# The experts of a mixture layer taken in an order computed on the chip, with the first pass taken out of the loops

## The reference, cut to what matters

```python
def moe_ffn(h, w_router, b_router, w_gate_up, b_gate_up, w_down, b_down):
    logits = (xt @ w_router + b_router).astype(jnp.float32)
    top_val, top_idx = lax.top_k(logits, TOP_K)              # 4 of 32
    gates = jax.nn.softmax(top_val, axis=-1)
    ...
    def expert_block(args):
        xb, e = args
        gu = xb @ w_gate_up[e] + b_gate_up[e]                # 1024 -> 2048
        gate = jnp.minimum(gu[:, :D_FF], SWIGLU_LIMIT)
        up = jnp.clip(gu[:, D_FF:], -SWIGLU_LIMIT, SWIGLU_LIMIT)
        act = (up + 1) * gate * jax.nn.sigmoid(gate * SWIGLU_ALPHA)
        return act @ w_down[e] + b_down[e]                   # 1024 -> 1024
    ...
    out = jnp.zeros_like(xt).at[sorted_tok].add(contrib)     # times the gate
```

## Time and profile before

| what | before |
|---|---|
| median of three runs | 1321.47 us (1320.93 to 1327.84) |
| profiled execution | 1323.31 us |
| its span in the trace | 1321.6 us |
| TensorE busy | 1251.1 us, 95% |
| VectorE busy | 488.0 us, 37% |
| ScalarE busy | 251.9 us, 19% |
| GpSimd busy | 43.6 us, 3% |
| moved by DMA | 436.31 MB |

### The profile page before, as it was taken

The page is one execution under the profiler, slowest core; times in us unless marked ns, Lnnn a source line. Parts: engine busy times, 40 slices in busy tenths (PEclk is TensorE's granted clock), DMA queues, the critical chain, the costliest instruction groups (busy, mean ns, idle before and its releaser), DMA issues.

```text
span 1321.6 us, 17005 instructions
## 1 busy us (share of the span) xinstructions
PE 1251.1 (95%) x6399; PEld 545.0 (41%) x6400; DVE 488.0 (37%) x961; ACT 251.9 (19%) x440; POOL 43.6 (3%) x66
## 2 busy tenths in 40 slices
PE   5999999997999999999999999998899999999996
PEld 4665654653433343334333433333333333343332
DVE  2623544465423342334233432232233223342334
ACT  2031124462111111111111111111111111111112
POOL 2000003402000000000000000000000000000000
PEclk9989999997999999999999999999999999999998
DMA  9513126135999566994999999999999988999994
GB/s 322 205 64 129 64 80 215 42 127 216 427 428 428 234 282 271 429 428 194 429 428 428 428 428 428 428 428 428 428 428 428 428 343 362 429 428 428 428 428 201
DMA packets 43400, 436.31 MB, mean 330 GB/s; under 512 B 5717, under 2 KB 6861, under 8 KB 18806
## 3 DMA queue, kind: packets, MB, share of 16 engines
q1 hardware_dynamic: 39376, 429.41, 77.8%
q0 software_dynamic: 2080, 6.48, 1.5%
q10 hardware_dynamic: 1926, 0.18, 0.1%
HBM read 432.33 MB, written 3.72 MB: 330 GB/s over the span
## 4 chain that ended last, share of the span: by engine, by line
PE 70%; DMA 25%; DVE 3%; issue 1%; ACT 0%; ACTq 0%; SPq 0%; DVEq 0%
PE PS L1739 28%; DMA ring<-in_w_gate_up_dram 24%; PE PS L1774 12%; PE PS L1259 7%; PE PS L1268 5%; PE PS L1701 4%; PE PS L1221 3%; PE PS L1673 3%; PE PS L1270 1%; PE PS L1555 1%; PE PS L1727 1%; PE PS L1529 1%; PE PS L1410 1%; PE PS L1396 1%; DMA gffn<-in_norm_ffn_g_dram 1%
## 5 line engine op out<-in xcount | busy, mean ns | idle before, releaser
L1739 PE MATMUL PS<-ring,r 128*64 128x512 f32 x2304 | 523.5, 598 | 30.6 <-DMA ring<-in_w_gate_up_dram 30.6
L1739 PEld LDWEIGHTS PS<-ring,r 128*64 128x64 f32 x2304 | 158.6, 137 | 337.9 <-issue 274.2
L1774 PE MATMUL PS<-ring,r 128*64 128x512 f32 x1152 | 255.1, 595 | 0.2
L1134 DVE SCALAR_TENSOR_TENSOR r<-PS,gprev,r 128x512 f32<-128x512 f32 (+1 forms) x222 | 152.4, 741 | 119.3 <-PE PS L1701 119.3
L1774 PEld LDWEIGHTS PS<-ring,r 128*64 128x64 f32 x1152 | 82.2, 137 | 148.2 <-issue 148.2
L1200 DVE TENSOR_TENSOR yy<-PS,yy 128x512 fp32r<-128x512 f32 x36 | 24.9, 692 | 253.2 <-ACT yy L731 253.2
L722 ACT ACTIVATE r<-r 128x512 f32<-128x512 f32 x36 | 22.7, 630 | 492.0 <-DVE r L1186 492.0
L1186 DVE TENSOR_SCALAR r<-PS 128x512 f32<-128x512 f32 x36 | 24.9, 692 | 233.1 <-PE PS L1739 233.1
L1221 PE MATMUL PS<-ident,r 128*128 128x128 f32 (+5 forms) x490 | 81.6, 297 | 14.3 <-DMA gffn<-in_norm_ffn_g_dram 11.9
L1259 PE MATMUL PS<-r,ring 128*128 128x323 f32 x320 | 88.9, 435 | 0.2 <-DVE r L769 0.2
L1221 PEld LDWEIGHTS PS<-ident,r 128*128 128x128 f32 (+5 forms) x490 | 62.2, 183 | 39.6 <-issue 19.7
(11 more groups left out here) (293 smaller groups left out, 763.7 us busy)
## 6 DMA issues: line engine op xcount, KB each, us to landing
ring<-in_w_gate_up_dram SPq DMA_DIRECT2D x128, 2048.0 KB, 18.2
ring<-in_w_down_dram SPq DMA_DIRECT2D x64, 2048.0 KB, 18.1
ring<-in_w_in_dram SPq DMA_DIRECT2D x8, 2048.0 KB, 18.4
ring<-in_w_out_dram SPq DMA_DIRECT2D x3, 2048.0 KB, 7.7
r<-in_x_prompt_dram SPq DMA_DIRECT2D x2, 512.0 KB, 4.0
r<-in_x_prompt_dram POOLq DMA_DIRECT2D x2, 512.0 KB, 5.1
r<-bias_table_clipped SPq DMA_DIRECT2D x4, 256.0 KB, 7.1
out_dram<-r SPq DMA_DIRECT2D x2, 512.0 KB, 2.7
```

The lines of the kernel that those rows point to most:

```text
L1134: v.scalar_tensor_tensor(xx, PS[0:rows, out_banks(t)[h], :], gprev[0:rows, t:t + 1], xx, ALU.mult, ALU.add)\
L1739: last = mm(PS[64 * h:64 * h + 64, m, :], xt[:, k % 4, k // 4, :], w[:, kk, D * m + 512 * h:D * m + 512 * h + 512], start=False, stop=(k = ...
L1774: last = mm(PS[64 * h:64 * h + 64, 2, :], at[:, kk, c, :], w[:, kk, 512 * h:512 * h + 512], start=(c == 0 and kk == 0), stop=(c == 1 and k ...
```

## The change

Five edits stand in it.

1. **Order of the experts.** VectorE computes a key for each expert and its rank among the keys (`turn_no`). With m experts of more than 64 tokens (`many`; m = `many_to` at its end), the i-th expert that has not more gets the key i (m + 1), the j-th that has more gets j (33 - m) + 0.5, and expert 0 gets 0. One matmul with `ones` brings blocks and numbers of the experts into the order of the turns (`by_turn`); `order` holds the expert of each turn, `before` now the blocks before each turn, `turn_of` the turn of each block. SyncE's loop reads `order[n]` and `before[n]`; TensorE waits for the weights by turn.
2. **First pass outside the loops.** On TensorE, VectorE and ScalarE the loop's body is a function, and its first pass is written out with constants (expert 0, block 0). TensorE no longer waits for `route_ready` ahead of it. In this pass `combine` stands behind the third chunk instead of the first, and the transposes of the tables (three rows now) and of the gates stand behind the first and the second chunk. `gathered(0)` on VectorE moves ahead of the tables' second half, and `route_ready` comes ahead of the gates.
3. **Casts.** `top_four` compares with the integer indices themselves; `ix` is gone.
4. **Small loads.** `gffn4` is loaded behind the bias table, and counts on `head_in`.
5. **Start.** VectorE normalises the first two row tiles ahead of `par`, and TensorE transposes the first tile ahead of the wait for `gain_in`.

The diff, cut to its core (scratch views of `spare`, semaphore names and buffers are left out):

```diff
@@ -44,7 +44,7 @@
 EXPERT_SLOT = (1, 2, 3, 4, 0, 5)
-N_GAIN, N_HEAD, N_LATE = 7, 5, 4
+N_GAIN, N_HEAD, N_LATE = 6, 6, 4
 PART_ROWS = (0, 64, 96)
@@ -320,8 +330,9 @@
             used = ["gs_used", "gs_used1", "gs_used2", "gu_mm", "ds_used", "d_mm"]
-            with sp.Fori(1, NE) as e:
-                first = sp.value_load(before[0:1, bass.ds(e, 1)], min_val=1, max_val=MAX_BLOCKS)
+            with sp.Fori(1, NE) as n:
+                e = sp.value_load(order[0:1, bass.ds(n, 1)], min_val=0, max_val=NE - 1)
+                first = sp.value_load(before[0:1, bass.ds(n, 1)], min_val=1, max_val=MAX_BLOCKS)
                 for c in range(GU_CHUNKS + DN_CHUNKS):
@@ -470,7 +481,6 @@
             gain(praw[40:88, :], conv_w[0].rearrange("j (k p) -> (j k) p", p=128))
-            gain(gffn4[:, :, :], norm_ffn_g[0].rearrange("(h p k) -> p h k", h=2, p=128))
             act.dma_start(hraw[0:3], state_conv[0, 0]).then_inc(s["cvhist_in"], 16)
@@ -483,6 +493,7 @@
             head(tab[:, :], rel_bias_table[0])
+            head(gffn4[:, :, :], norm_ffn_g[0].rearrange("(h p k) -> p h k", h=2, p=128))
             head(wdt[:, :, :], w_in[0].rearrange("(k p) n -> p k n", p=128)[:, :, C_DT:C_DT + HEADS])
@@ -715,9 +726,8 @@
             a.activation(place[:, 0:TC], PS[:, 4, 0:TC], ACT.Copy).then_inc(s["c_ready"], 1)
-            act.wait_ge(s["route_ready"], 1)
-            total = act.value_load(blocks[0:1, 0:1], min_val=NE, max_val=MAX_BLOCKS)
-            with act.Fori(0, total) as b:
+            def expert_pass(b):
...
                 act.wait_ge(s["g_ready"], b + 1)
@@ -729,6 +739,12 @@
                 a.activation(yy2[:, 0, :], bank(2), ACT.Copy).then_inc(s["yy_ready"], 1)
...
+            expert_pass(0)
+            act.wait_ge(s["route_ready"], 1)
+            total = act.value_load(blocks[0:1, 0:1], min_val=NE, max_val=MAX_BLOCKS)
+            with act.Fori(1, total) as b:
+                expert_pass(b)
             for t in range(NT):
@@ -761,10 +774,14 @@
             normalised(0)
+            normalised(1)
+            dve.wait_ge(s["par_mm"], 1)
+            v.tensor_copy(par[:, :], PS[:, 7, 0:88]).then_inc(s["par_ready"], 1)
+            dve.wait_ge(s["par_ready"], 1)
             for i in range(6):
                 t, h, rows = i // 2, i % 2, ROWS[i // 2]
-                if h == 0 and t + 1 < NT:
-                    normalised(t + 1)
+                if i == 2:
+                    normalised(2)
                 dve.wait_ge(s["hT_mm"], i + 1)
@@ -1051,9 +1068,8 @@
                 step(v.max_index(i8[:, t, :], m8[:, t, :], lg[:, t, :]))
-                step(v.tensor_copy(ix[:, t, :], i8[:, t, :]))
                 step(v.tensor_tensor(eq[:, t, :, :], bc(iota[:, 0:NE].unsqueeze(1), 128, TOPK, NE),
-                                     bc(ix[:, t, 0:TOPK].unsqueeze(2), 128, TOPK, NE), ALU.is_equal))
+                                     bc(i8[:, t, 0:TOPK].unsqueeze(2), 128, TOPK, NE), ALU.is_equal))
                 for at0 in range(0, 128, rows):
@@ -1138,18 +1154,47 @@
-            count, nb, upto = PS[:, 2, 0:NE], nbk[:, 0, :], nbk[:, 1, :]
-            step(v.tensor_scalar(nb, count, float(CAP), 1.0, ALU.is_gt, ALU.add))
+            count, key, nb = PS[:, 2, 0:NE], key_nb[:, 0, :], key_nb[:, 1, :]
+            step(v.tensor_scalar(many, count, float(CAP), None, ALU.is_gt))
+            step(v.tensor_scalar(nb, many, 1.0, None, ALU.add))
             for m in range(2, TC // CAP):
                 step(v.scalar_tensor_tensor(nb, count, float(CAP * m), nb, ALU.is_gt, ALU.add))
-            step(v.tensor_tensor_scan(upto, nb, nbk[:, 3, :], 0.0, ALU.add, ALU.add))
-            step(v.tensor_scalar(nbk[:, 2, :], upto, pidx[:, 0:1], None, ALU.is_le))
-            step(v.tensor_tensor(nbk[:, 3, :], nbk[:, 2, :], nb, ALU.mult))
-            step(v.tensor_reduce(bej[:, :], nbk[:, 2:4, :], axis=X, op=ALU.add))
+            step(v.tensor_tensor_scan(many_to, many, zeros32, 0.0, ALU.add, ALU.add))
+            step(v.tensor_scalar(n_few, many_to[:, NE - 1:NE], -1.0, float(NE + 1), ALU.mult, ALU.add))
+            step(v.tensor_scalar(n_many, many_to[:, NE - 1:NE], 1.0, None, ALU.add))
+            step(v.tensor_tensor(few, rank[:, 0:NE], many_to, ALU.subtract))
+            step(v.tensor_scalar(few, few, n_many, None, ALU.mult))
+            step(v.tensor_scalar(key, many_to, n_few, 0.5, ALU.mult, ALU.add))
+            step(v.tensor_tensor(key, key, few, ALU.subtract))
+            step(v.tensor_tensor(key, key, many, ALU.mult))
+            step(v.tensor_tensor(key, key, few, ALU.add))
+            step(v.memset(key[:, 0:1], 0.0))
+            step(v.tensor_tensor(own, key_nb, bc(ident[:, 0:NE].unsqueeze(1), 128, 2, NE), ALU.mult))
+            step(v.tensor_reduce(own_key, own, axis=X, op=ALU.add))
+            step(v.tensor_scalar(few, key, own_key[:, 0:1], None, ALU.is_lt))
+            step(v.tensor_reduce(turn_no, few, axis=X, op=ALU.add))
+            step(v.tensor_scalar(at_turn[0:NE, 0, :], iota[0:NE, 0:NE + 1], turn_no[0:NE], own_key[0:NE, 1:2],
+                                 ALU.is_equal, ALU.mult))
+            v.tensor_scalar(at_turn[0:NE, 1, :], iota[0:NE, 0:NE + 1], turn_no[0:NE], pidx[0:NE],
+                            ALU.is_equal, ALU.mult).then_inc(s["turns_ready"], 1)
+            gathered(0)
+            dve.wait_ge(s["turns_mm"], 1)
+            step(v.tensor_copy(by_turn, PS[:, 2, 64:66 + 2 * NE].rearrange("p (a e) -> p a e", a=2)))
+            step(v.tensor_tensor_scan(upto, by_turn[:, 0, 0:NE], zeros32, 0.0, ALU.add, ALU.add))
+            step(v.tensor_tensor(few, by_turn[:, 1, 1:NE + 1], by_turn[:, 1, 0:NE], ALU.subtract))
+            step(v.tensor_scalar(done[:, 0, :], upto, pidx[:, 0:1], None, ALU.is_le))
+            step(v.tensor_tensor(done[:, 1, :], done[:, 0, :], by_turn[:, 0, 0:NE], ALU.mult))
+            step(v.tensor_tensor(done[:, 2, :], done[:, 0, :], few, ALU.mult))
+            step(v.tensor_reduce(bej[:, :], done, axis=X, op=ALU.add))
             v.tensor_tensor(bej[:, 1:2], pidx[:, :], bej[:, 1:2], ALU.subtract).then_inc(s["bej_ready"], 1)
-            step(v.tensor_tensor(nb[0:1], upto[0:1], nb[0:1], ALU.subtract))
-            step(v.tensor_copy(before[:, :], nb[0:1]))
+            step(v.tensor_tensor(few[0:1], upto[0:1], by_turn[0:1, 0, 0:NE], ALU.subtract))
+            step(v.tensor_copy(before[:, :], few[0:1]))
+            step(v.tensor_copy(order[:, :], by_turn[0:1, 1, 0:NE]))
             step(v.tensor_copy(blocks[:, :], upto[0:1, NE - 1:NE]))
+            dve.wait_ge(s["bej_mm"], 1)
+            step(v.tensor_scalar(turn_of[:, :], PS[0:1, 7, 0:128], float(NE - 1), None, ALU.min))
+            step(v.tensor_scalar(place_of[:, :], PS[0:1, 7, 128:256], 0.0, None, ALU.max))
+            v.tensor_copy(expert_of[:, :], PS[0:1, 7, 256:384]).then_inc(s["route_ready"], 1)
             dve.wait_ge(s["pv_ready"], 1)
@@ -1158,21 +1203,17 @@
             step(v.tensor_copy(pg[:, :, NT:2 * NT].rearrange("p e t -> p t e"), gates4[:, :, 0, :]))
-            dve.wait_ge(s["bej_mm"], 1)
-            step(v.tensor_scalar(expert_of[:, :], PS[0:1, 7, 0:128], float(NE - 1), None, ALU.min))
-            v.tensor_scalar(place_of[:, :], PS[0:1, 7, 128:256], 0.0, None, ALU.max).then_inc(s["route_ready"], 1)
             dve.wait_ge(s["route_ready"], 1)
             dve.sem_inc(s["o_ev"], 2)
-            gathered(0)
-            total = dve.value_load(blocks[0:1, 0:1], min_val=NE, max_val=MAX_BLOCKS)
             dve.wait_ge(s["c_ready"], 1)
...
             dve.sem_inc(s["yyl_ready"], 1)
-            with dve.Fori(0, total) as b:
-                e = dve.value_load(expert_of[0:1, bass.ds(b, 1)], min_val=0, max_val=NE - 1)
...
+            def expert_pass(b, e):
...
                 e_next = dve.value_load(expert_of[0:1, bass.ds(b + 1, 1)], min_val=0, max_val=NE - 1)
@@ -1199,6 +1240,11 @@
                     .then_inc(s["yyl_ready"], 1)
...
+            expert_pass(0, 0)
+            total = dve.value_load(blocks[0:1, 0:1], min_val=NE, max_val=MAX_BLOCKS)
+            with dve.Fori(1, total) as b:
+                expert_pass(b, dve.value_load(expert_of[0:1, bass.ds(b, 1)], min_val=0, max_val=NE - 1))
             dve.wait_ge(s["gates_held"], total + 2)
@@ -1222,11 +1268,11 @@
-            pe.wait_ge(s["gain_in"], N_GAIN * 16)
-            tr(PS[:, 7, 0:88], praw[:, :]).then_inc(s["par_mm"], 1)
...
             for i in range(6):
                 t, h, rows = i // 2, i % 2, ROWS[i // 2]
+                if i == 2:
+                    pe.wait_ge(s["gain_in"], N_GAIN * 16)
+                    tr(PS[:, 7, 0:88], praw[:, :]).then_inc(s["par_mm"], 1)
                 pe.wait_ge(s["xnorm"], t + 1)
@@ -1703,22 +1751,21 @@
-            gather(0)
-            pe.wait_ge(s["bej_ready"], 1)
-            for c in range(2):
-                last = tr(PS[0:1, 7, 128 * c:128 * c + 128], bej[:, c:c + 1])
-            last.then_inc(s["bej_mm"], 1)
-            turn(0)
-            places(0)
```

(39 more changed lines are left out.)

27 lines of the change are left out of this document (18 added, 9 removed).

## The result

| | before | after |
|---|---|---|
| median, first comparison (4 runs each) | 1322.76 us | 1309.17 us (1307.18 to 1309.51) |
| ratio, with its 95% interval | | 0.9888 (0.9858 to 0.9919) |
| the same again, 7 runs before and 4 after | 1325.39 us | 1309.58 us, ratio 0.9892 (0.9873 to 0.9911) |
| the same again, 9 runs before and 4 after | 1326.11 us | 1309.10 us, ratio 0.9876 (0.9858 to 0.9894) |
| profiled execution, span | 1323.31, 1321.6 us | 1308.86, 1307.1 us |

The change is a gain of 1.1 to 1.2%. The sign and the way in which the order works came as predicted, the size did not: 20.3 us were predicted, 14.5 us lie between the two spans, and 1309.2 us is outside the range, which ended at 1306.5.

A forecast was written before the change was run, and what follows sets the result against it. The prediction saw two limits, TensorE at 26.5 us a block and DMA at 29.4 us an expert. Order -20.5 and later first refill +0.2 gave -20.3, from 1321.5 to 1301.2 us; range 1296 to 1306.5.

The forecast's parts named there:

- What bounds it; the order: Expert passes: TensorE 26.5 us a block, DMA 29.4 us an expert; each two-block expert's second block frees five passes.
- The term of 20.5 us: Expert passes: spreading the two-block experts cuts losses from 36.4 to 15.9 us, saving 20.5 us.
- so passes 1 to 5 are free: Start of the expert passes: pass 0 counts as a second block, so passes 1 to 5 lose nothing.
- From R to pass 5, 2.7 us: First weight refill to pass 5's sigmoid: 142.5 us, taken from an earlier refill at 612.19, putting the sigmoid at 463.8.
- R, 1.2 us: Pass 0: first weight refill at 321.3, later than before's 320.55, although pass 0 starts 2.1 us earlier.
- 0.3 three times: Bound on the order's losses in the expert passes: +-0.3 us per cycle, three times.
- The start of the program: First projection: starts at 18.5, set by weight chunk 0; 0.5 us saved, between 0 and 0.6.
- The router: Removed casts on VectorE: the comparison is held behind GpSimd on the shared port, so only 0.2 us is gained.
- rival (a): Router: the comparison is not held, everything up to the first refill comes 1.8 us earlier, 1299.4 us; 10%.
- (b): Pass 0: first refill over 4 us late through slow first reads or a slow new chain, 1306 us and more; 7%.
- (c): Expert order: the turns don't move the doubled experts or lead can't be spread; 36.4 us stay, 1321.7 us; 5%.
- (d): SyncE's loop: two dependent reads per expert don't fit in 3.5 us, each us beyond delaying 31 refills; slower, 2%.

The follow-up runs named there:

- natural: Changed kernel with only the expert order undone (keys are the experts' numbers): 1324.70 us against 1325.11 for the kernel before, ratio 0.9995.
- gfin_late: Changed kernel with the final norm's gain (0.5 MB) fetched at pass 7 instead of pass 0: 1307.38 us, one run.
- gfin_end: Changed kernel with the final norm's gain fetched in pass 34 instead of pass 0: 1307.91 us, 0.9886 of the kernel before.
- order_only: Changed kernel with the first pass back in the loops, tables and gates transposed ahead of it: 1311.19 us, 0.9912 of the kernel before.
- same_again: The changed kernel unaltered, profiled once more: 1308.64 us, one run.
- after_timed: The changed kernel unaltered, timed again in four runs: 1309.58 us, 0.9892 of the kernel before.
- the fillers: Fourteen transposes nobody reads, added to the changed kernel in TensorE's wait before the first projection: 1304.80 us, 0.9847 of the kernel before.
- gfin_half: Changed kernel with the final norm's gain fetched at pass 7 and the tables transposed inside chunk 0: 1307.03 us, 0.9870 of the kernel before.
- warm: Changed kernel with thirty unread transposes in TensorE's gaps of the router and the gathering: 1312.53 us, one run.
- start_warm: Changed kernel with fourteen unread transposes in TensorE's wait before the first projection, a single look: 1303.86 us, one run.
- start_timed: The same fourteen unread transposes before the first projection of the changed kernel, timed in four runs: 1304.80 us, 0.9847 of the kernel before.
- tables_half: Changed kernel with the tables transposed inside chunk 0 of pass 0 instead of behind it: 1307.78 us, one run.

## Why the prediction was wrong, step by step

p35 was predicted at 1275.0 (a span of 1301.3 less the 26.3 behind it) and stood at 1280.84, 5.8 us later (most of it is seen again in the 15.7 us that the order is worth by natural, for 20.5). The three distances of the table divide them: 1.2 before R, 2.7 from R to pass 5, 1.9 behind it.

**What bounds it; the order. Right in kind.** The doubles moved to their turns, and the five free passes behind them and the losses at 12, 13, 20, 21, 28 and 29 came as told, but for the chance loss at 19. The term of 20.5 us was the one mis-sized: 15.7 by natural. The step that failed is "so passes 1 to 5 are free". It counted pass 0 as a double, since both have the refill 10.44 us ahead of the sigmoid, and checked pass 5 with the landings of 612.19. Passes 4 and 5 lost 3.2 us: they must be paid for by a punctual first refill, and the margin there was 0.3 us.

**From R to pass 5, 2.7 us: the term that failed most.** I took 142.5 us from the refill of 612.19. Measured: 145.1 to 145.2 in every unaltered profile, of which 1.5 to 1.6 is the fetch of `gfin` (shown by gfin_late, gfin_end and order_only). In before it was issued at 314.77, ahead of the first refill; the change moved the refills' neighbour, and I never costed where that load went. The other 1.0 us is the model row. At 612.19 the first two chunks land 5.3 us apart; at the first refill 6.0 us in gfin_late and 6.3 in gfin_end, with nothing beside them. Before's own first refill had 6.3 too, and could have been read. It isn't that they are put in the queue together: they are 0.9 us apart there in gfin_end, but 4.7 in before and in order_only, where they land 6.3 and 6.6 apart. Why the first refill takes longer is open.

A third limit hid behind these two. Pass 1's sigmoid stood at 358.43, 0.9 us behind before's 357.51 and not within 0.5. Four passes of 26.51 us from there end at 464.47, where natural's pass 5 stood (464.42) with no wait for weights. So even a punctual refill would have given pass 5 at 464.4 and not at 463.8.

**R, 1.2 us.** Pass 0 began at 312.48 (312.65 predicted), which is luck: VectorE's chain began at 306.21 instead of 307.1 and took 5.6 us instead of 4.8. TensorE's chunk 0, VectorE's first conversion and its third:

```profile
313.31 5.93 PE L1790 MATMUL PS<-ring,r 128*64 128x512 f32 x16
```
```profile
319.78 0.28 DVE L1195 TENSOR_SCALAR turn_of<-PS 1x128 int32<-1x128 f32 x1 [4.62 <-PE PS L1267]
...
320.40 0.28 DVE L1197 CAST expert_of<-PS 1x128 int32<-1x128 f32 x1
```

and two windows of the same stretch:

```profile
310.00:314.00 4.00, 3.09 (x14) 1.81 (x14) 3.37 (x14) 0.00 (x0) 0.00 (x0) 0.50 0.00 0
314.00:318.00 4.00, 4.00 (x12) 1.25 (x10) 0.99 (x7) 0.00 (x0) 0.00 (x0) 0.50 0.00 0
```

Chunk 0 ended at 319.24 instead of 318.2, since the clock came back only at 318 us, when all but the last 1.2 us of the chunk was done. Chunk 0 had begun 2.3 us earlier than before's (315.58), but the clock came back when before's did, at 317.9: at 4.79 us the sum had taken before's mix of both levels, and 5.93 was nearly all at the lower. VectorE waited 4.62 us for the tables as told, and SyncE's two reads took 322.51 - 320.68 = 1.8 instead of 1.5 us. In all four unaltered profiles R is 3.26 us behind the end of chunk 0, for 3.0 predicted. What moves R among them is when pass 0 begins and at which clock: in same_again chunk 0 took 4.47 us, but began 1.0 us later.

**Behind pass 5, 1.9 us.** 1.21 is the chance loss at pass 19; the rest is that the first losses of the three cycles were 2.5 to 2.8 and not 2.3 to 2.5. In after_timed, which had no chance loss, the stretch took 811.67 us for the 811.2 of the prediction. The bound of "0.3 three times" left no room for chance losses, which stand in eight of the nineteen profiles taken with the change in some form.

**The start of the program: no gain.** The projection began at 17.66, not 18.5, and 1.4 us ahead of before's, and still it ended at 71.88 for before's 71.63. Its 192 matmuls took 54.22 us in after and 52.59 in before: in after they ran at half the clock up to 21.0 us, in before at the full one from the start, 0.17 us behind the transposes of x. The gap that the earlier transposes left is 1.35 us in after and 2.57 in after_timed. That the gap costs the clock is argued from this and not shown: the fillers were to close it, and with them too the projection began at the lower clock. M came 0.24 to 1.24 us later than before's in three of four unaltered profiles and 0.68 earlier in the fourth. Before has one profile alone, so the sign isn't shown; the 0.5 us predicted did not appear.

**The router: rule right, size wrong.** VectorE in the kernel after:

```profile
296.90 0.29 DVE L1071 TENSOR_TENSOR r<-iota,i 128x128 f32<-128x128 f32 x1
...
297.63 1.59 DVE L1113 TENSOR_TENSOR r<-chosen 128x32 f32<-128x32 f32 x1
...
301.04 1.60 DVE L1117 TENSOR_TENSOR expo<-lg,m 128x96 f32<-128x96 f32 x1
```

and GpSimd:

```profile
296.99 2.19 POOL L452 TENSOR_TENSOR r<-r 128x1024 f32<-128x1024 f32 x1 [13.36 <-ACT r L688]
...
300.41 2.12 POOL L456 TENSOR_TENSOR r<-r 128x1024 bf16<-128x1024 f32 x1 [1.23 <-ACT r L692]
```

The comparison was not held: it began 0.09 us ahead of GpSimd and took 0.29. That is no accident of this profile; in all nineteen it begins 0.08 to 0.10 us ahead, where before's cast had begun 0.07 behind. The next instruction with two SBUF inputs, L1113, was: 1.59 us for what took 0.19, ending 0.04 behind GpSimd's. So the wait moved two instructions down, as the page "SBUF — State Buffer" of the Trainium skill (section "SBUF: two separate sides") has it: who starts first keeps the port to the end of its instruction. The comparison and its reduction were through by then, and the tables' chain began at 306.21 instead of 307.76, 1.55 us earlier and not 0.2: 1.12 by the end of L1117, and 0.43 by work behind it, where the CAST of `sel` (L1136, L1120 before) took 0.19 instead of 1.15 us, since it began 0.58 us ahead of GpSimd's next instruction and not 0.15 behind. So rival (a)'s condition came true, and its size nearly, by another road than it had named; the longer chain behind ate half of it, and R was late for other reasons.

**The rivals.** (b), a first refill late by over 4 us because of slow reads or a slow chain, did not come: R was 1.2 us late, mostly by the clock. The time that it names, 1306 and more, was met through losses that it does not mention, above all those between R and pass 5. (c) and (d) did not come either: natural shows the order working, and the refills between doubles are 26.51 us apart, with no trace of SyncE's second read.

## What to carry to other kernels

When a resource is spread so evenly that every stage has just its margin, cost the first stage as closely as the last: a delay that the old, uneven order forgave is now paid in full, and each transfer that shares the queue there needs its own line in the sum. Put loads that nothing needs soon where the DMA is idle, not merely later: moved within a DMA-bound stretch they seem to cost the same. And when TensorE starts earlier, read where it ends and at which clock: here 1.4 us gained ahead of a long row of matmuls were lost again inside it. An edit can also pay at a place far from where it stands: fourteen idle transposes at 16 us brought next to nothing by the end of the row behind them and 1.5 us at 76, so read several marks along the way before you say what an edit did.

## What the runs showed of the hardware

- The clock at a start depends on the execution: the same kernel's chunk 0 took 4.47, 5.88, 5.93 and 6.17 us, and one profile (gfin_half) had no drop at 76 to 84 us where all others had. By itself that makes the way from the projection's end to M 3.2 us shorter (27.8 for 31.0).
- The clock drops at 76 us although TensorE is busy all the time (4.00 of 4 us in the windows at 76 and 80 us), in before too.
- In the first profile of the kernel after the granted clock reads 1.00 from 18 to 21 us, yet the projection's matmuls begin 0.54 us apart there, as in after_timed, where it reads 0.50, and 0.27 apart behind 21.0. The first record of the clock in this trace stands at 21.0 us; ahead of the first record a 1.00 says nothing, and the distance of equal matmuls decides.
- From M to the first weight matmul of pass 0 four unaltered and five altered profiles (warm, start_warm, start_timed, tables_half, gfin_half) agree within 0.03 us (210.46 to 210.49), though M goes from 99.35 to 104.06. Such a stretch is a good ruler: what is added there shows at once.
- A DMA-bound cycle of seven experts loses 5.1 to 5.7 us, and in some executions 1.2 to 1.6 us more, at a place that changes. The chunks' landings show such a place in the first profile of the kernel after, at 730 us: 6.6 us from one landing to the next, between neighbours of 4.9. What takes it is open; no load but the weights was under way there.
